# A loop over 32 experts on one core: a weight load reordered, a scaling moved to GpSimd, and small vector work moved forward

## What is computed

```python
x = layer_norm(DN_ALPHA * x + m, ln1_g[i], ln1_b[i])
f = hier_moe(x, ...)
x = layer_norm(DN_ALPHA * x + f, ln2_g[i], ln2_b[i])

def hier_moe(x, ...):
    # a router gives each token 2 of 32 experts and two gate weights
    def block(args):                      # rows of one expert
        hdn = silu(xb @ w1[e]) * (xb @ w3[e])
        return (hdn @ w2[e]) * w[:, None]
```

## Time and profile before

| | us |
|---|---|
| median of 3 runs | 2996.56 |
| lowest and highest run | 2993.69, 2999.35 |
| time of the profiled execution | 2994.94 |
| span of the profiled execution | 2993.1 |
| TensorE busy in it | 2895.8 |
| VectorE busy | 2123.5 |
| ScalarE busy | 1604.9 |
| GpSimd busy | 358.4 |

### The profile page before, as it was taken

How to read it: one execution, slowest core, us unless ns; L and a number is a source line. 1 busy time by engine, 2 the same in 40 slices (tenths; PEclk the granted TensorE clock), 3 DMA queues, 4 the chain that set the end, 5 groups by cost and what they waited for, 6 DMA issues and landing times.

```text
span 2993.1 us, 38811 instructions
## 1 busy us (share of the span) xinstructions
PE 2895.8 (97%) x14261; PEld 2257.0 (75%) x14261; DVE 2123.5 (71%) x2376; ACT 1604.9 (54%) x1969; POOL 358.4 (12%) x273
## 2 busy tenths in 40 slices
PE   8999899999989999899999999999999999999998
PEld 7668776767768767677677668888888887888886
DVE  3485799999972467899999865674776648676762
ACT  3573588888853464788888743433222226522211
POOL 0000212222220002122222220100000000000000
PEclk9999899999999998999999999999999999999999
DMA  7303799999962125899999844301232223232222
GB/s 273 136 1 113 261 389 405 409 398 400 405 223 85 39 99 226 334 399 398 404 399 406 332 106 99 66 20 64 92 102 95 99 85 99 92 111 93 91 94 84
DMA packets 170900, 600.50 MB, mean 201 GB/s; under 512 B 21697, under 2 KB 71025, under 8 KB 121363
## 3 DMA queue, kind: packets, MB, share of 16 engines
q1 hardware_dynamic: 140432, 541.22, 48.5%
q0 software_dynamic: 19840, 52.60, 4.9%
q10 hardware_dynamic: 10499, 4.91, 0.6%
HBM read 574.15 MB, written 40.37 MB: 205 GB/s over the span
## 4 chain that ended last, share of the span: by engine, by line
PE 73%; DMA 11%; DVE 7%; ACT 5%; issue 3%; POOL 1%; DVEq 0%; SPq 0%; ACTq 0%; POOLq 0%
PE bank L2074 14%; PE bank L2076 14%; PE bank L2075 14%; DMA ring<-w_gate 6%; PE bank L2512 4%; PE bank L2509 4%; DMA ring<-w_up 3%; PE bank L2086 3%; PE bank L2794 2%; PE bank L2528 2%; PE bank L2081 2%; PE bank L2082 2%; PE bank L2138 1%; PE bank L2139 1%; ACT ring_rounded L1479 1%
## 5 line engine op out<-in xcount | busy, mean ns | idle before, releaser
L3601 DVE TENSOR_TENSOR ring_rounded<-ring,big_rounded 128x2048 fp32r<-128x2048 f32 x252 | 567.6, 2288 | 32.0 <-ACT big_rounded L1479 31.0
L1479 ACT ACTIVATE big_rounded<-ring 128x2048 fp32r<-128x2048 f32 x252 | 481.9, 1916 | 44.2 <-DMA ring<-w_up 33.2
L3096 DVE TENSOR_TENSOR ring_rounded<-ring,ring_rounded 128x2048 fp32r<-128x2048 f32 (+2 forms) x118 | 261.4, 2255 | 329.8 <-ACT ring_rounded L1221 329.4
L1221 ACT ACTIVATE ring_rounded<-ring 128x2048 fp32r<-128x2048 f32 (+2 forms) x124 | 226.5, 1876 | 369.3 <-DMA ring<-ffn_w_down 150.1
L3601 DVE TENSOR_TENSOR ring_rounded<-ring,ring_rounded 128x2048 fp32r<-128x2048 f32 x128 | 292.4, 2288 | 43.5 <-ACT ring_rounded L1479 43.1
L1479 ACT ACTIVATE ring_rounded<-ring 128x2048 fp32r<-128x2048 f32 x128 | 245.0, 1917 | 96.5 <-DMA ring<-w_gate 95.5
L2074 PE MATMUL bank<-XT_rounded,ring_rounded 128*128 128x512 f32 (+1 forms) x792 | 295.8, 374 | 0.4 <-DVE XH_rounded L3149 0.4
L2076 PE MATMUL bank<-XT_rounded,ring_rounded 128*128 128x512 f32 (+1 forms) x792 | 292.9, 370 | 0.0
L2075 PE MATMUL bank<-XH_rounded,ring_rounded 128*128 128x512 f32 (+1 forms) x792 | 292.9, 370 | 0.0
L2512 PE MATMUL bank<-ring_rounded,big_rounded 128*128 128x512 f32 x960 | 265.7, 399 | 7.4 <-DVE ring_rounded L3601 6.9
L2075 PE MATMUL bank<-ring_rounded,XH_rounded 128*64 128x512 f32 (+2 forms) x608 | 239.6, 394 | 0.0
(11 more groups left out here) (525 smaller groups left out, 5527.1 us busy)
## 6 DMA issues: line engine op xcount, KB each, us to landing
ring<-w_up SPq DMA_DIRECT2D x128, 1024.0 KB, 9.8
ring<-w_down SPq DMA_DIRECT2D x128, 1024.0 KB, 7.7
ring<-w_gate SPq DMA_DIRECT2D x128, 1024.0 KB, 7.9
ring<-ffn_w_up SPq DMA_DIRECT2D x44, 1024.0 KB, 7.0
ring<-ret_gdn_w_in SPq DMA_DIRECT2D x8, 2048.0 KB, 13.1
ring<-ffn_w_down SPq DMA_DIRECT2D x8, 2048.0 KB, 7.7
expert_rows<-lnp POOLq DMA_DIRECT2D x1, 12288.0 KB, 40.3
ring<-odd_w_qkv SPq DMA_DIRECT2D x6, 2048.0 KB, 8.1
```

What stands on the lines that cost most here:

```text
L1221: act.activation(one_pass(hi(c)[:, ks, :]), raw(c)[:, ks, :], ACT.Copy).then_inc(rounded[c.pair], 1)
L1479: act.activation(one_pass(expert_hi(j)), expert_raw(j), ACT.Copy).then_inc(signal("half_rounded").sem, 1)
L3096: dve.tensor_tensor(one_pass(w), w, parts(hi(c)[:, ks, :]), ALU.subtract).then_inc(split[c.pair], 1)
L3601: dve.tensor_tensor(one_pass(expert_raw(j)), expert_raw(j), parts(expert_hi(j)), ALU.subtract).then_inc(signal("half_split").sem, 1)
```

## The change

Four things, in each of the two layers:

- SyncE loads expert 2's down halves ahead of expert 3's gate and up.
- The multiplication of X by ALPHA goes to GpSimd, behind gather(1) and ahead of gather(2). VectorE waits for it (`x_scaled`) behind the last expert.
- `bounds` moves into `stage_0`, ahead of `hidden(0, 0)`.
- `gate_weights` moves into `stage_1`, between `hidden(1, 1)` and `hidden_T(1, 1)`.

```diff
                 next_gate_up(0)
                 next_down(1)
                 next_gate_up(1)
+                next_down(2)
                 next_gate_up(2)
-                next_down(2)
                 with sp.Fori(3, EXPERTS - 1) as e:
...
                 gather(1)
+                for t in range(T):
+                    pool.tensor_scalar(X[:, t, :], X[:, t, :], ALPHA, None, ALU.mult).then_inc(signal("x_scaled").sem, 1)
                 for e in range(EXPERTS):
...
                     for j in GATE + UP + DOWN[0:1]:
                         rest_of_half(0, j, early=True)
+                    bounds(l)
                     hidden(0, 0)
...
                     hidden(1, 1)
+                    gate_weights(l)
                     hidden_T(1, 1)
...
                 stage_0()
                 stage_1()
-                dve.wait_ge(signal("rows_sent").sem, signal("rows_sent").next(dve, 16 * T * TOP_K))
-                for t in range(T):
-                    dve.tensor_scalar(X[:, t, :], X[:, t, :], ALPHA, None, ALU.mult).then_inc(dve_done.sem, 1)
-                    dve.wait_ge(dve_done.sem, dve_done.next(dve))
-                bounds(l)
-                gate_weights(l)
                 stage(2, 0, down=False)
...
                 stage(EXPERTS - 1, 1, last=True)
+                dve.wait_ge(signal("x_scaled").sem, signal("x_scaled").next(dve, T))
```

## The result

| | before | changed |
|---|---|---|
| median of 6 runs, us | 2993.81 (2992.48 to 2999.35) | 3006.38 (3005.26 to 3008.00) |
| ratio to before, 95% interval | | 1.0037 (1.0026 to 1.0048) |
| profiled execution, us | 2994.94 | 3008.00 |
| its span, us | 2993.1 | 3006.2 |

The change makes the kernel slower by 12.6 us, and the interval does not hold 1. By the ratio, which is not that of the two medians, the loss is 0.37%, 11.1 us. The prediction was 3006.8 us. Three more runs of the kernel before lowered its median by 2.75 us, so the forecast difference was +10.2 us against a measured +12.6, or +11.1 by the ratio.

What follows compares the result with a forecast made beforehand. DMA and TensorE were taken as both full mid-stage, so front delays stay. Per layer 4.16 + 0.30 + 1.6 - 0.95 + 0.6 - 0.7 = +5.0 us, second +5.2; +10.2 on 2996.6 gave 3006.8 us, range 2992 to 3013.

Steps and rivals of the forecast that it cites:

- GpSimd's scalings: Stage 0: four scalings on GpSimd hold VectorE ahead of `hidden(0, 0)`, 1.04 us each, +4.16 us a layer.
- The fourth: Last GpSimd scaling, in stage 0: meets `bounds` and costs VectorE 0 to 1.04 us, taken as 1.04.
- `bounds`, +0.30: Stage 0, ahead of `hidden(0, 0)`: of its 2.06 us, VectorE's idle time covers 1.76; +0.30 us a layer.
- `gate_weights`, 0: Stage 1, ahead of `hidden_T(1, 1)`: its 1.64 us are covered by TensorE's 1.62 us wait but for some 0.1; 0.
- The clock behind the late step: TensorE behind the longer gap before expert 0's down: matmuls at a low granted clock, +1.6 us a layer.
- The load order: Down halves ahead of expert 3's gate: delay its load, +0.6 us; expert 4's queue empties sooner, -0.7, a layer.
- expert 3's gap: TensorE's wait at expert 3: with VectorE free, `hidden(2)` starts when the silu ends, -0.95 us a layer.
- The sum: All terms: +5.0 us in the first layer, +5.2 in the second, together +10.2 us; this case's chance 0.52.
- A: Rival, stage 0: GpSimd's scaling does not hold the port, or runs only in VectorE's idle time; -1.5 us, chance 0.27.
- B: Rival: if A holds, earlier down halves also remove TensorE's gap at expert 5's gate; -7.9 us, chance 0.15.
- C: Rival, stage 0: scalings much slower (1.9 us each) or the low clock lasts longer; +17 us, chance 0.06.
- D: Rival within the main case: only three scalings count and down halves cost gate nothing; +6.7 us, no separate chance.

Runs made afterwards that it cites:

- e1: The change, but with X scaled by VectorE behind the last expert instead of by GpSimd; 2996.70 us, ratio 1.0011 to the kernel before.
- e2: The change, but with X scaled by VectorE in stage 0 just ahead of `bounds` instead of by GpSimd; 3004.84 us, ratio 1.0040 to the kernel before.
- e3: e1 plus four GpSimd memsets of XT where the change has the scalings; 2996.77 us, ratio 1.0010 to the kernel before.
- experiment 1: The run of e1, 2996.70 us; the six kernels named there, the kernel before among them, have nothing new in stage 0.
- e6: The kernel before with only `bounds` and `gate_weights` moved to stages 0 and 1; 2993.69 us, ratio 1.0000.
- e5: The kernel before with only the load order changed, expert 2's down ahead of expert 3's gate and up; 2997.19 us, ratio 1.0012.
- e8: The kernel before with only X's four scalings moved behind the last expert, still on VectorE; 2991.39 us, ratio 0.9992.
- e4: The change, but with GpSimd's four scalings one by one at experts 12 to 15; 2997.29 us, ratio 1.0015 to the kernel before.
- e9: The kernel before with only expert 2's first down half moved ahead of expert 3's gate and up; 2994.32 us, ratio 1.0005.
- e10: e8, with ScalarE also taking expert 2's silu ahead of rounding expert 3's first gate half; 2989.31 us, ratio 0.9986 to the kernel before.
- e7: The kernel before with only X's scaling moved to GpSimd, at the change's place; 2995.31 us, ratio 1.0004.

## Why the prediction was right, point by point

**GpSimd's scalings, +4.16 predicted.** The mechanism held (e1, e2, e3). The size is 0.84 us for each of three splits and 0.86 for the one operation of `bounds`: 3.38 us. I had charged a full GpSimd instruction, 1.04, for each. The fourth, for which I had no row and took the upper end, did come. What I expected of GpSimd itself was wrong: 1 to 2 us for a scaling, where four took 12.98, 3.24 each, three times both of my estimates (1.04 and 0.88). What VectorE loses to one is near them all the same.

**`bounds`, +0.30, and `gate_weights`, 0.** `hidden(0, 0)` of e1 is 0.2 us late against layer 1 of the kernel before, and 0.6 against the average of the six kernels named in experiment 1; e6 is at 1.0000. The term held in size, but its cover of 1.76 us, read from one execution, is near the upper end of 0.45 to 1.82. `gate_weights` costs a little: with it the first matmul of expert 1's down comes 2.90 us after `hidden(1, 1)` starts (e1, e6), and without it 2.63 or 2.64 (e5, e8 and layer 2 before). Layer 1 before, from which I read a cover of 1.62 us, has 3.08 and is the exception.

**The clock behind the late step, +1.6.** Mis-sized: 15 matmuls in 6.13 us are 2.8 lost, in both layers. I had taken the loss behind a gap of 1.62 us for one of nearly three times its length. With the terms above, layer 1's delay at `hidden(1, 1)` is 3.65 + 2.8 = 6.45, as the table has it, where I had 4.46 + 1.6 = 6.1. The errors of the two terms cancel in part.

**The load order, +0.6 - 0.7, and expert 3's gap, -0.95.** This is the step that failed in its sign: the three terms are -1.05 us together, and from the issue of expert 3's gate to that of expert 4's the change is 0.4 and 1.2 us slower. The load of expert 3's gate is 1.3 us slower (e5: 1.6), double my value though within the bounds, and this takes the gain of 0.95: from the issue of gate to `hidden(2)` pass 9.7 us in layer 1 and 10.5 in layer 2, against 9.3 before. e6 and e8, which keep the old load order, have 8.3 to 8.7, so the 0.95 was there to be had. Expert 4's gate did come 1.1 us sooner, better than my 0.7, but it does not make up for it: e5 costs 0.12% alone, 1.8 us a layer, where I had some -0.1. The part of the change that looks most like a repair is a loss, since it puts 1 MB ahead of the very transfer that releases the silu.

**The sum.** Predicted +5.0 and +5.2; the table has +5.3 and +6.5 at `combine`, and 1.3 us lies elsewhere. That it is so near is luck in part. The delay reaches 6.7 and 8.2 us at expert 4's gate, and the 1.4 and 1.7 us that are then made up have no term in the prediction, which held that a delay at the front is not caught up; this cancels most of the wrong sign of the load order. The median difference is 12.6 against 10.2, and the time forecast is nearly exact only because the first median of before was 2.75 us high.

**The rivals.** A (the port is not held) fell with 9.21 us. B (faster through expert 5's gate) fell with it. C was near: its low clock did last longer, but its scalings were not dearer to VectorE. D (the delay is smaller) did not come either: the fourth scaling counted, and the down halves did cost gate something.

## What to carry to other kernels

Before work is moved to a place where an engine is idle, add up all that is moved there against that idle time; here either part overran 1.76 us by less than 1 us and both together by 3.65, and behind the longer gap the low clock added 2.8 us. Read that idle time from more than one execution and layer: it was 0.45 to 1.82 us here. A late step at the front of a stage in which DMA and TensorE are both full is paid for the most part, while the same disturbance in its middle (e4) cost nothing that could be measured. When an engine waits for a load, do not put another load shortly in front of that one (e5, e9). Whether it pays to take what is on the path out from behind the load (e10) the measurement does not tell.

## What the hardware showed that I had not expected

A scaling of 128x1024 on GpSimd takes 3.24 us beside VectorE's splits, and 2.80 to 4.80 where it stands alone among them (e4), yet it takes only 0.84 us from a split in stage 0 and 0.85 to 1.50 from a run of three in e4. It looks as if the rest were waiting for VectorE's splits, but e7 speaks against that. There the fourth scaling runs from 332.04 to 335.11, the last split ends at about 332.4, VectorE is idle from 333.07 to 334.41, and the scaling takes 3.07 us all the same. Even an operation on 128x8 can be held, for 0.86 us. In the changed kernel it is the one of `bounds` that falls into the last 1.0 us of the fourth scaling (334.38 to 335.38; in layer 2 at the same place); the eight in front of it, which ran beside the same scaling, kept their length but for 0.07 us in one. So the rows look as if a scaling keeps VectorE out only during the last 0.85 us or so of its 3; that was not tested.

The low clock also comes and goes with nothing changed. Timeline of TensorE in e1, the first matmul of expert 1's down in layer 1 and in layer 2:

```profile
354.90 0.71 PE L2074 MATMUL bank<-big_rounded,XH_rounded 128*96 128x512 f32 x1 [1.45 <-DVE XH_rounded L3615]
...
1211.97 0.47 PE L2074 MATMUL bank<-big_rounded,XH_rounded 128*96 128x512 f32 x1 [1.45 <-DVE XH_rounded L3615]
```

Both gaps are 1.45 us long; in the 3.60 us behind the first the granted clock is 0.53 (9 matmuls), behind the second 1.00 (16 matmuls). From `hidden(1, 1)` to the issue of expert 3's gate pass 12.24 us in the one layer and 10.71 in the other, as 12.42 and 11.99 before and 10.39 in e8's first. In all the profiled executions this stretch falls into two groups, 10.4 to 10.7 us and 12.0 to 12.4, and the kernel of the load order alone has one layer in each. What decides between them was not tested. These 1.5 us are as large as a part's effect here, so one profile cannot rank such parts; the ratios have to.
